# Final norm and stores ahead of the overflow branch, the squares of the first mixer norm inside layer 2, and transposes tile by tile

## The reference, cut to what matters

```python
x = first_block(...)                 # two trunk layers; each ends in
#   x_new = layer_norm(ALPHA * x + gate * out, post_g, post_b)
h = rmsnorm(x, mix_norm)             # x * rsqrt(mean(x*x) + eps) * g
z = h @ w_in                         # q, k, v, f_logit, gate_in, rec_in
x = x + concat([att, lru_out]) @ w_out
h2 = rmsnorm(x, ffn_norm)
y = hierarchical_moe(h2, ...)        # 4 groups x 8 experts, top 2 in one group
return rmsnorm(x + y, final_norm)
```

## Time and profile before

| | us |
|---|---|
| median of 3 runs | 1412.73 |
| lowest and highest | 1411.54, 1414.36 |
| the profiled execution, own time | 1413.81 |
| its span in the trace | 1412.0 |

### The profile page before, as it was taken

The page is one execution under the profiler, slowest core; times in us unless marked ns, Lnnn a source line. Parts: engine busy times, 40 slices in busy tenths (PEclk is TensorE's granted clock), DMA queues, the critical chain, the costliest instruction groups (busy, mean ns, idle before and its releaser), DMA issues. The chain is left out here.

```text
span 1412.0 us, 19330 instructions
## 1 busy us (share of the span) xinstructions
PE 1323.9 (94%) x7954; PEld 1005.2 (71%) x7954; DVE 630.1 (45%) x1093; ACT 527.0 (37%) x885; POOL 67.2 (5%) x92
## 2 busy tenths in 40 slices
PE   5999989899999999999989889999999989999996
PEld 2777666676788888878866679998676566666663
DVE  2323564566233343478346875667413152222212
ACT  2356334444723232325563566443234121111112
POOL 0000002231000000011000230000000000000000
PEclk7999989999999999999999999999999999999998
DMA  9522120327122252224331103563331859999980
GB/s 386 195 82 90 64 116 31 149 91 269 60 90 90 94 203 91 90 98 146 126 117 60 61 31 135 191 216 145 108 119 60 357 201 380 397 415 403 419 362 32
DMA packets 34222, 238.97 MB, mean 169 GB/s; under 512 B 4304, under 2 KB 4432, under 8 KB 6224
## 3 DMA queue, kind: packets, MB, share of 16 engines
q1 hardware_dynamic: 34128, 237.66, 43.7%
HBM read 236.59 MB, written 1.05 MB: 168 GB/s over the span
## 5 line engine op out<-in xcount | busy, mean ns | idle before, releaser
L229 DVE TENSOR_TENSOR pieces_lo<-weight_ring,pieces_hi 128x1024 fp32r<-128x1024 f32 x154 | 187.7, 1223 | 283.0 <-ACT pieces_hi L221 282.7
L247 PE MATMUL proj<-h_hi,pieces_hi 128*128 128x512 f32 (+1 forms) x816 | 290.3, 356 | 5.9 <-DVE h_lo L1145 2.9
L248 PE MATMUL proj<-h_lo,pieces_hi 128*128 128x512 f32 (+1 forms) x816 | 284.9, 349 | 0.0
L249 PE MATMUL proj<-h_hi,pieces_lo 128*128 128x512 f32 (+1 forms) x816 | 283.4, 347 | 0.0
L221 ACT ACTIVATE pieces_hi<-weight_ring 128x1024 fp32r<-128x1024 f32 x158 | 165.3, 1053 | 95.9 <-PE score L249 50.7
L247 PEld LDWEIGHTS proj<-h_hi,pieces_hi 128*128 128x128 f32 x816 | 156.1, 191 | 36.8 <-issue 10.1
L248 PEld LDWEIGHTS proj<-h_lo,pieces_hi 128*128 128x128 f32 x816 | 156.3, 192 | 21.7 <-issue 2.0
L249 PEld LDWEIGHTS proj<-h_hi,pieces_lo 128*128 128x128 f32 x816 | 156.1, 191 | 20.2
L1943 PE MATMUL turn<-expert_parts,e_gathered 128*64 128x256 f32 x768 | 85.3, 379 | 0.8 <-DVE e_gathered L2132 0.8
L1943 PEld LDWEIGHTS turn<-expert_parts,e_gathered 128*64 128x64 f32 x768 | 55.9, 137 | 32.4 <-issue 7.3
L1078 ACT ACTIVATE l_merge_gate<-proj 128x512 f32<-128x512 f32 (+1 forms) x48 | 23.5, 490 | 125.4 <-PE proj L249 125.4
(11 more groups left out here) (440 smaller groups left out, 2033.8 us busy)
## 6 DMA issues: line engine op xcount, KB each, us to landing
weight_ring<-in_stream SPq DMA_DIRECT2D x110, 1024.0 KB, 4.8
expert_parts<-in_experts SPq DMA_DIRECT2D x70, 1024.0 KB, 11.0
weight_ring<-in_experts SPq DMA_DIRECT2D x26, 1024.0 KB, 11.0
l_rows<-in_rows SPq DMA_DIRECT2D x2, 768.0 KB, 15.6
l_y_attn<-in_ada_first SPq DMA_DIRECT2D x1, 1024.0 KB, 5.2
l_y_gla<-in_ada_first SPq DMA_DIRECT2D x1, 1024.0 KB, 7.3
l_y_sgu<-in_ada_first SPq DMA_DIRECT2D x1, 1024.0 KB, 8.2
l_q<-in_ada_first SPq DMA_DIRECT2D x1, 1024.0 KB, 10.1
```

Source lines behind the costliest of these rows:

```text
L229: eng.tensor_tensor(self.part(self.lo_ring[:, n % NPIECE, :], kind), self.raw(slot, c, kind), self.part(self.hi_ring[:, n % NPIECE, :], ki ...
L247: pe.matmul(out, sh, mh, start=start, stop=False)
L248: pe.matmul(out, sh, ml, start=False, stop=False)
L249: return pe.matmul(out, sl, mh, start=False, stop=stop)
```

## The change

It has five parts.

1. **The first mixer norm's squares and roots go into layer 2** (step `square`, at the end of its list). ACT waits for a new signal `x_posted` for each tile; the scratch output goes to `mT`, the sums to a new tensor `fixed` (576 bytes in each partition). `fixed` also holds a copy of the identity and of the mixer norm's weights, loaded by two new DMAs at the start of layer 2 (64 KB and 4 KB). PE's products that nobody reads at the end of layer 2 become 42 in place of 30. The four products of that kind at the start of the mixer are gone.
2. **PE transposes tile by tile.** The eight blocks of the first tile wait for the first scaling alone, the eight of the second for the second. DVE, PE and ACT no longer wait for the mixer's own parameters there; PE waits for them at `f`, DVE at `rec`.
3. **A root at the mixer's end** on one column of `par`, by ACT, with nothing that reads it; one more like it (`root_warm`) behind ACT's last work of the experts' main part.
4. **Routing.** DVE's step `rank` is split: `choose` comes ahead of the second tile's `rows`. The first `sel` is written in two halves, and the first pair of gathers waits for the first half only.
5. **The end.** The final norm and its stores are written ahead of the overflow branch, and once more inside its body. DVE writes to a new place (`FO`, over the old `hT`) instead of in place; the second tile is computed and stored in two halves (three stores: 512, 256 and 256 KB). SP's load of the flag and its branch now come behind the three stores and ahead of its wait for them.

```diff
@@ trunk_schedule
+    if l:
+        return steps + [("post_a", 3), ("post_b", 2), ("post_b", 3), ("square", 2), ("square", 3)]
@@ trunk_layer, PE
-            keep_busy(pe, bank.tile(free), HH[:, 0, :], 512, 8 if l == 0 else 30)
+            if l:
+                pe.wait_ge(*sig.fixed_in.at(32))
+            keep_busy(pe, bank.tile(free), HH[:, 0, :], 512, 8 if l == 0 else 42)
@@ trunk_layer, ACT
+                elif kind == "square":
+                    t = i - 2
+                    st = fixed[:, F_ST:F_ST + 8]
+                    act.wait_ge(*sig.x_posted[t].at(1))
+                    link(act.activation(mT[:, 2 * t:2 * t + 2, :].rearrange("p a c -> p (a c)"), xres(i), ACT.Square,
+                                        scale=D ** -0.5, accum_out=st[:, t:t + 1]))
+                    act.activation(st[:, 4 + t:5 + t], st[:, t:t + 1], ACT.Sqrt, bias=eps).then_inc(*sig.norm_root.one())
@@ trunk_layer, SP
+                sp.dma_start(fixed[:, F_ID:F_ID + P], io["mixer_params"][:, M_ID:M_ID + P]).then_inc(*sig.fixed_in.dma())
+                sp.dma_start(fixed[:, F_NORM1:F_W], io["mixer_params"][:, M_NORM1:M_NORM1 + KT]).then_inc(*sig.fixed_in.dma())
@@ mixer, PE
-                    acc = PJ.open(pe, J("turnx", i))
                     if i == 0:
-                        keep_busy(pe, acc, xlat[:, 0, :], 512, 3)
+                        accs = [PJ.open(pe, J("turnx", n)) for n in range(4)]
                         pe.wait_ge(*sig.scaled.at(1))
-                        keep_busy(pe, acc, xlat[:, 0, :], 512, 1)
-                        pe.wait_ge(*sig.small_in.at(32))
+                        for k in range(KT):
+                            pe.transpose(accs[k // 2][:, k % 2 * T:k % 2 * T + P], XS[:, 0, k * P:(k + 1) * P], ident)
                         pe.wait_ge(*sig.scaled.at(2))
-                    for n in range(4):
-                        k, t = 2 * i + n // 2, n % 2
-                        last = pe.transpose(acc[:, n * P:(n + 1) * P], XS[:, t, k * P:(k + 1) * P], ident)
+                    for k in (2 * i, 2 * i + 1):
+                        last = pe.transpose(accs[i][:, k % 2 * T + P:(k % 2 + 1) * T], XS[:, 1, k * P:(k + 1) * P], ident)
                     last.then_inc(*PJ.done())
@@ mixer, ACT
-                if kind == "norm":
-                    link(act.activation(XS[:, i, :], xlat[:, i, :], ACT.Square, scale=D ** -0.5, accum_out=st[:, i:i + 1]))
...
+            act.activation(st[:, 7:8], par[:, M_EPS:M_EPS + 1], ACT.Sqrt)
@@ experts
-        main_work += [("rows", 0), ("rows", 1), ("route", 0), ("route", 1), ("rank", 0)] + MAIN_STEPS
+        main_work += [("rows", 0), ("route", 0), ("route", 1), ("choose", 0), ("rows", 1), ("rank", 0)] + MAIN_STEPS
@@ experts, first sel in halves; gather
+                    n = E // 2 if i == 0 else E
+                    for e in range(0, E, n):
...
-                    pe.wait_ge(*sig.selected.at(q // 2 + 1))
+                    pe.wait_ge(*sig.selected.at(q // 2 + 2 if q else 1))
@@ experts, the end: DVE
+            vector_steps(dve, main_work)
+            dve.engine_nop().then_inc(*sig.x_done.one())
+            dve.wait_ge(*sig.fin_in.at(16))
+            final_rows(dve, link, 0)
             with dve.register("dve_over") as r:
...
@@ experts, the end: SP
             EW.issue(sp, 6 * PAIRS)
+            final_stores(sp, 0)
             sp.wait_ge(*sig.over_flag.at(1))
             with sp.register("sp_over") as r:
                 sp.reg_load(r, FLAGI[0:1, 0:1])
                 with sp.If_ne(r, 0):
+                    sp.wait_ge(*store.at(16 * len(stores)))
                     EW.issue(sp, 6 * ROUNDS * PAIRS)
-            for t in range(2):
...
+                    final_stores(sp, 1)
+                    sp.wait_ge(*store.at(32 * len(stores)))
+            sp.wait_ge(*store.at(16 * len(stores)))
```

More of the change, by code:

```diff
@@ L331, in __init__ @@
         self.context_done = signal("context_done")
+        self.fixed_in = signal("fixed_in")
+        self.x_posted = [signal(f"x_posted{t}") for t in range(2)]
         self.hc_f32 = signal("hc_f32")
@@ L1425, in mixer_schedule, with mixer @@
     return steps + [("out", g) for g in (2, 3, 1, 4, 5, 6, 7)]
-def mixer(nc, io, W, EW, jobs, sig, par, xlat):
+def mixer(nc, io, W, EW, jobs, sig, par, xlat, fixed):
     T = M_TOK
@@ L2184, in _ @@
                 with dve.If_ne(r, 0):
+                    dve.wait_ge(*store.at(16 * len(stores)))
                     vector_steps(dve, OVER_STEPS)
-            dve.engine_nop().then_inc(*sig.x_done.one())
-            dve.wait_ge(*sig.fin_in.at(16))
-            for t in range(2):
-                dve.wait_ge(*sig.norm_root.at(t + 2))
-                link(dve.reciprocal(st[:, 6 + t:7 + t], st[:, 6 + t:7 + t]))
-                dve.scalar_tensor_tensor(xlat[:, t, :], xlat[:, t, :], st[:, 6 + t:7 + t], fin[:], ALU.mult, ALU.mult)\
-                    .then_inc(*sig.norm_out.one())
+                    dve.engine_nop().then_inc(*sig.x_done.one())
+                    final_rows(dve, link, 1)
         @block.sync
```

76 lines of the change are left out of this document (48 added, 28 removed).

## The result

| | before | changed |
|---|---|---|
| median of 5 runs, us | 1411.54 | 1405.43 |
| lowest and highest | 1411.44, 1414.36 | 1404.54, 1406.39 |
| the profiled execution, own time | 1413.81 | 1404.54 |
| its span | 1412.0 | 1402.8 |

The ratio is 0.995, with a 95% interval from 0.9937 to 0.9963: the change gains 6.1 us, where 5.05 were forecast. Timed again, the changed kernel gave 1406.95 (5 runs) beside 1412.94 for the kernel before (17 runs), ratio 0.9959 [0.9946, 0.9972]. The first median, 1405.43, lies just under the range given; the second lies inside it.

A forecast was written before the change was run, and what follows sets the result against it. PE, busy 94% of the span, was taken as the bound, with savings where it waits on short DVE, ACT and sequencer chains. Terms 2.1 + 0.55 + 2.4 = 5.05 us off 1412.73 gave 1407.7 us, range 1405.6 to 1409.6.

The forecast's parts named there:

- Layer 2 into the mixer: From layer 2's end to the mixer's first projection: projection starts at 995.85 in place of 998.01, gain 2.1 us.
- Routing: Experts' routing: earlier choice gives 0 behind PE's filler, half select cuts the gather's wait from 1.18 us; gain 0.55 us.
- the mirror that the prediction gave the filler: Routing's filler ahead of `rank`: its time can move by up to 0.7 us either way with when the clock falls.
- The end: Final norm, stores and SP's branch: stores leave earlier, but SP's branch (3.2 us) is then last; gain 2.4 us.
- the branch is free: Rival at the kernel's end: SP's branch costs nothing and the stores bound it; 1.5 us more gain, 1406.2 us; chance 0.17.
- The clock falls at the mixer's start: Rival: PE's idle time at the mixer's start drops the clock, losing 1.4 us; gain 3.6, 1409.1 us; chance 0.15.
- The sum: Whole kernel: 2.1 + 0.55 + 2.4 = 5.05 us off 1412.73, giving 1407.7 us.
- Slower by the weights: Rival in the experts' stage: moved SBUF places slow weight transfers, 1414.7 us at 7.5%; chance 0.03 with other causes.

The follow-up runs named there:

- sp_early: Changed kernel with SP's flag load and branch ahead of the stores, other engines' branches still behind the norm; median 1406.07 us, ratio 0.9951.
- old_turns: Changed kernel with only PE's transposes back in the old order, all behind the second scaling; median 1409.31 us, ratio 0.9971.
- old_turns_two_stores: Changed kernel with transposes in the old order and the second tile computed and stored whole (two stores, not three); executed once, 1409.38 us.
- old_turns_busy: Changed kernel with transposes in the old order plus three unread products ahead of the first scaling's wait; median 1406.39 us, ratio 0.9949.
- before_filler4: Kernel before with four unread products ahead of the rank products in place of six; executed once, 1413.54 us.

## Why the prediction was off

The direction and the places were right, and between the two profiles first compared the three terms were right to 0.1 us. What failed is the size of one term, the routing's, because a mechanism was missing from it, and with it the sum, which was taken from one profile.

- **Layer 2 into the mixer**: 2.1 forecast, 2.2 measured. The block's start was reckoned at 10.2 us behind the filler's first product and came at 10.0; DVE began on the first group 0.42 us behind the second tile's transposes, as reckoned.
- **Routing**: 0.55 forecast, 0.5 measured in the wait of the gather (0.65 in place of 1.18), and the choice gave 0 because the filler ends last. This is the step that failed: the half select was priced by its wait alone, and nothing was reckoned for the clock behind that wait. In the runs the clock never fell behind the half select's wait and fell in four of eight profiles behind the whole one's, for 1.5 us each. Mixer and head together gave 1.7 us on the mean where the sum had 0.55. The part of it that comes from the mixer's stretch has no known cause. And the mirror that the prediction gave the filler, "up to 0.7 either way", is too small: 1.7 in the changed kernel.
- **The end**: 2.4 forecast, 2.5 measured in the first pair of profiles and 2.4 on the mean of all. SP's branch was last, as forecast. Three sizes around it were off: the branch took 2.65 us and not 3.2, the load of the flag 0.75 and not 0.48, and the last landing came 3.4 us behind its issue, not 2.5. The first two nearly make up for each other; the third doesn't reach the sum, since the branch is last. But the rival "the branch is free" was priced at 1.5 us, and sp_early gave 0.47.
- **The clock falls at the mixer's start**: it didn't in the changed kernel. Its price was about right: 1.4 given, and 1.5 to 1.7 in the start of old_turns and old_turns_two_stores once the 0.25 of the order is off. The mixer behind it was another 1.6 to 1.8 longer there, but also in old_turns_busy, whose clock hadn't fallen.
- **The sum**: it was taken from one profile, on the assumption that what one execution's clock does stands for before and after alike. That profile had mixer and head at 157.0 us, where four others with the same code there have 158.5 to 158.7. So 5.05 became 2.2 + 1.7 + 2.4 = 6.3 on the mean. Of the 2.2 us between 1407.7 and 1405.43 this explains 1.2. The other 1.0 is within the noise: single executions of before scatter by 1.8 us (standard deviation of 33), so a median of three is uncertain by about 1 us, and the changed kernel's two medians lie 1.5 apart. That the first of them fell 0.17 us outside the range and the second inside is chance. The 6.3 rests on the places in the profiles alone: by the two intervals of the ratio the gain is 5.2 to 8.9 us and 4.0 to 7.6, which don't part it from 5.05. A range of 4 us should have had more room for this.
- **Slower by the weights**: main is 245.6 to 245.8 us in every profile. The change doesn't touch it.

## What to carry to other kernels

Before a saving of a few us is added up, profile the unchanged kernel two or three times and cut the profiles at the same places: what moves there by itself is not the change's. Where PE waits, the length of one idle gap can count twice, once as the wait and once as the clock behind it. Real work given to PE sooner shortened the start by more than filler did (13.4 against 14.7 us). A filler in front of a chain must be cut again when the chain gets shorter, or the gain stays hidden behind it.

## What the hardware showed that was not expected

- PE's idle gap and the clock: after 2.29 and 3.96 us idle at the mixer's start the granted clock fell to 0.50 each time (three profiles), after 1.43 never (seven). With the old start, where the longest gap was 1.64 to 1.67 us and products that nobody reads followed it, it never fell there either (eight). After 1.18 us ahead of the gather it fell in half of the profiles with six products of filler or four, after 0.65 never. The stretch that followed was 3.4 us.
- A branch that is taken costs far more than its row. SP's shows 50 ns and is followed by 2.65 us in which nothing stands on the engine (2.5 to 3.0 in the other profiles with the branch behind the stores); PE's row in before shows the whole of it, 3.43 us. The Trainium skill ("Runtime: NRT & Kernel Launch", section "Instruction fetch mechanics") says that a taken branch out of the pages held waits for a fetch. The traces agree for PE. In all 19 one packet of 16 KB on the queue for instructions starts 1.0 us behind the start of PE's branch, and the branch is longer where the packet is: 3.33 us with 1.01 in before_filler4, 3.43 with 1.09 in before, 3.87 with 1.47 in old_turns_two_stores. For SP no packet could be told from those of the other engines, so there the fetch is argued.
- The landing of the last stores took 3.4 us for 256 KB and 3.5 us for 512 KB (sp_early and old_turns_two_stores; 3.35 to 3.5 in every profile with the new end), where the two stores of the kernel before took 2.6. Why wasn't tried.
